# The decay matrices of a DeltaNet head in a lane of their own, with two pairs of tiles, and two tiles for the normed q

## The chip, the core and the metric

The kernel runs on one core of a Trainium2 chip. The metric is the device time of the core in microseconds (us); less is better. The engines named here are TensorE (PE; its weight loads are PEld), VectorE (DVE), ScalarE (ACT), GpSimd (POOL) and SyncE (SP), whose queue issues the DMAs.

## The reference, cut to what matters

Two transformer blocks on 512 tokens of width 1024, all in float32. Only the first block matters here. It runs grouped attention of 8 heads and, beside it, a bidirectional gated DeltaNet of 8 heads of 128, in chunks. Of one DeltaNet head and one direction (forward, and backward on the flipped sequence), with g the running sum of the log decays in a chunk:

```
decay  = exp(where(tril, g[:, None] - g[None, :], -inf))
L      = tril((k_beta @ k.T) * decay, -1)
T      = inverse of (I + L)                      # unit lower triangular
u, w   = T @ v_beta, T @ (k_beta * exp(g))
a      = (q @ k.T) * decay
# then over the chunks, one after the other
v_new  = u - w @ state
o      = (q * exp(g)) @ state + a @ v_new
state  = state * exp(g_last) + (k * exp(g_last - g)).T @ v_new
```

q and k are l2-normed, after a short convolution over the tokens and a silu.

## The kernel before

All operands are feature-major tiles of 128 x 512 (one "tile" below: 128 partitions, 512 columns, float32). A plain product of weights and activations is a `gemm` of 8 blocks; a block is three matmuls of 128x512 (step `mul`), high and low halves of both sides. 16 blocks, that is 48 `mul`, use one pair of weight tiles; the next pair is split on ACT and DVE meanwhile, and the load of the pair after that (1 MB) goes out on SP once that is done.

The function `arrange` writes one order of steps for all engines. It keeps a clock per engine from a table of costs and a list of lanes (Python generators). Between two `mul` it lets each lane whose time has come add its next step; if a product can't go on, lanes are forced. Every engine then runs its steps strictly in that order, with semaphores between the engines. So a step that is planned early on PE and whose operand is late holds all matmuls behind it.

The head loop of block 1 goes over `hd` = 0 to 7. Each turn has the products of k, the attention q, the DeltaNet q, the attention gate, v and two gates of the head before; its lanes are `att` (attention), `conv` and `con2` (convolution, silu and norm of k, q and v), `prep`, `scan` and `out`. The steps that matter, by name:

- `cv_r` i, `cv_n` i: PE sums the squares of a convolved tile (q for i = hd, k for i = 8 + hd), ACT makes the reciprocal root in two instructions, and DVE writes the normed tile (L2423): k into a tile kept by the head, q into the one tile `q_tile`.
- `g_ld` hd, d: SP loads the row of running sums of direction d, spread over the partitions, into `GS`. `pr_a`: ACT takes exp into `G_of[d]`. `pr_g`: DVE subtracts the column (4 instructions, L2432) into `B_of[d]`. `pr_e`: ACT takes exp of `B_of[d]`; POOL copies 4 columns (L3213), multiplies `q_tile` by `G_of[d]` into the kept tile `qe` (L3214), and masks `B_of[d]` (L3216).
- `pr_kk`: PE makes k k^T and q k^T (8 matmuls of 128x128 in the program, two records each in the trace); DVE multiplies both by the decays (2 and 8 instructions).
- `pr_b`, `lv_0`, then `lv_m` and `lv_x` for s = 1 to 4, `lv_e`, `lv_p1`, `lv_p2`, `lv_q1`, `lv_q2`: the triangular inverse by levels. `lv_m` and `lv_x` are 32 matmuls of 32x32 each (64 records). `lv_0` has POOL mask levels 0 and 1 (L3219, L3220); `lv_m` s < 4 has POOL mask level s + 1 (L3228), released by that `lv_m`. `lv_p1` and `lv_q1` read `B_of` once more. `lv_q2` is written back by DVE (L2487).
- `sc_v`, `sc_s`, `sc_r`, `sc_o`, `sc_oq`: the scan over four chunk pairs; POOL scales k for it (`sc_kd`, L3239). `on_b`: the norm behind it.

Before, one pair of tiles `B_of` and the one `q_tile` serve all heads. So `prep` of a head does all of `pr_a`, `pr_g`, `pr_e` itself, after both `cv_n` and after the head before has ended `lv_q2` (`work` is one slot), and only then `pr_kk`. The `cv_r` of the next q waits for `pr_kk` of the head before.

All matmuls stand at line 1833 and transposes at line 1836, since a helper records them.

Of the kernel before, what the change touches and what calls it, by code (L numbers as in the profile page):

```python
# [54 lines left out]
PRIORITY = {"tail": -2, "deca": -4, "silu": -3, "egat": -3, "att": -2, "conv": -1, "con2": -1, "scan": 0, "out": 1, "prep": 2, "gate": 3, "load": 4, "halv": 4,  # L55
# [179 lines left out]
def arrange(o, n_pairs):  # L235
# [310 lines left out]
    keep, work, acc, pads = Slots(2), Slots(1), Slots(2), Slots(4)  # L546
# [73 lines left out]
    def conv_lane(i, ip, t_in):  # L620
# [42 lines left out]
        if what == "q" and hd:  # L663
            o.behind(o.at["pr_kk", hd - 1])
# [14 lines left out]

    def prep_lane(hd):  # L680
# [9 lines left out]
        def add(kind, *key, cost, ring_=True, hold=False):  # L690
            st = banked(kind, *key, cost=cost, hold=hold) if ring_ else o.add(kind, *key, cost=cost)
            st.hd, st.keep, st.k_old, st.w_old = hd, ikeep, k_old, w_old
            return st

        for d in range(2):
            while ("g_ld", hd, d) not in o.at:
                yield
            o.behind(o.at["g_ld", hd, d])
            yield "DV"
            add("pr_a", hd, d, cost=[("AC", AC_B)], ring_=False)  # L700
            yield "DV"
            add("pr_g", hd, d, cost=[("DV", 4 * DV_S)], ring_=False)
            if hd < 7:
                t = o.now
                o.add("g_ld", hd + 1, d, cost=[("DMA", 4.0)])
                o.now = t
            yield
            add("pr_e", hd, d, cost=[("AC", AC_B), ("PO", PO_B), ("PO", PO_B)], ring_=False)
            yield "PE"
# [39 lines left out]
        work.give(0, st)  # L749

# [758 lines left out]
def build(nc, wstream, wba, consts, vecs, cossin, pos, xT, pT, outT):  # L1509
# [6 lines left out]
    with ctx:  # L1516
# [18 lines left out]
        NA = 41  # L1535
# [134 lines left out]
        B01 = A(18, 2).rearrange("p d (c n) -> p d c n", c=4)  # L1670
# [158 lines left out]
        def tensor(pe):  # L1829
# [9 lines left out]
            for q in steps:  # L1839
# [145 lines left out]
                elif kind == "pr_kk":  # L1985
                    hd = q.hd
                    w.wait_ge(sem("cv_n"), max(at["cv_n", hd].n, at["cv_n", 8 + hd].n))
                    kt_, qt_ = g4(keep_of[q.keep]["k"]), g4(q_tile)
# [28 lines left out]
                elif kind == "lv_p1":  # L2017
# [29 lines left out]
                elif kind == "lv_q1":  # L2047
# [6 lines left out]
                    for c in range(4):  # L2054
                        for d in range(2):
                            sr, ds = halves64(d)
                            i = mm(bb[ds, c, :], g4(B_of[d])[sr, c, ds], TA[sr, c, :], True, True)
# [34 lines left out]
                elif kind == "sc_oq":  # L2092
# [3 lines left out]
                    w.wait_ge(sem("pr_qe"), at["pr_e", hd, 1].n)  # L2096
# [169 lines left out]
        def vector(dve):  # L2266
# [14 lines left out]
            for q in steps:  # L2281
# [128 lines left out]
                elif kind == "cv_n":  # L2410
                    hd = q.hd
                    w.wait_ge(sem("cv_rs"), q.n)
                    if q.what == "q":
                        dst, scale = q_tile, 128.0 ** -0.5
                        if hd:
                            w.wait_ge(sem("pr_qe"), at["pr_e", hd - 1, 1].n)
                            full(at["pr_kk", hd - 1].u2)
# [7 lines left out]
                elif kind == "pr_g":  # L2425
# [5 lines left out]
                    for c in range(4):  # L2431
                        i = ts(g4(B_of[d])[:, c, :], g4(GS[:, d, :])[:, c, :], g3(gcol)[:, c, col:col + 1], 0.0,  # L2432
                               ALU.subtract, ALU.min)
                    i.then_inc(sem("pr_d"), 1)
                elif kind == "pr_kk":
# [5 lines left out]
                    for d in range(2):  # L2441
                        i = tt(K[f"AT{d}"], psum[q.u2.b][:, :], B_of[d], ALU.mult)
                    i.then_inc(drained[q.u2.b], 1)
                    empty(q.u2)
                    for d in range(2):
                        for c in range(4):
                            b_, col = g4(B_of[d])[:, c, :], d * 8 + hd
# [53 lines left out]
                elif kind == "sc_s":  # L2501
# [4 lines left out]
                    else:  # L2506
                        w.wait_ge(sem("pr_qe"), at["pr_e", hd, 1].n)
# [270 lines left out]
        def scalar(act):  # L2778
# [57 lines left out]
            for q in steps:  # L2836
# [123 lines left out]
                elif kind == "pr_a":  # L2960
                    hd, d = q.key
                    w.wait_ge(sem(f"g_ld{d}"), 16 * (hd + 1))
                    if hd:
                        w.wait_ge(sem("pr_qe"), at["pr_e", hd - 1, d].n)
                    f(G_of[d], GS[:, d, :], ACT.Exp).then_inc(sem("pr_eg"), 1)
                elif kind == "pr_e":
                    hd, d = q.key
                    w.wait_ge(sem("pr_d"), at["pr_g", hd, d].n)
                    f(B_of[d], B_of[d], ACT.Exp).then_inc(sem("pr_ed"), 1)
                elif kind == "pr_b":  # L2970
                    empty(q.u)
                    for r in Q32:
                        i = copy(dc32(hB)[r], B01[r, :, :, r])
# [219 lines left out]
        def gpsimd(po):  # L3193
# [6 lines left out]
            for q in steps:  # L3200
# [5 lines left out]
                elif kind == "pr_e":  # L3206
                    hd, d = q.key
                    LG, K, e0, D = G_of[d], keep_of[q.keep], (d * 8 + hd) * 4, B_of[d]
                    w.wait_ge(sem("pr_eg"), at["pr_g", hd, d].n)
# [3 lines left out]
                    po.tensor_copy(eglast[:, e0:e0 + 4], g4(LG)[:, :, 127 if d == 0 else 0])  # L3213
                    tt(K[f"qe{d}"], q_tile, LG, ALU.mult).then_inc(sem("pr_qe"), 1)  # L3214
                    w.wait_ge(sem("pr_ed"), q.n)
                    tt(g4(D), g4(D), bc4(C["tri_u" if d == 0 else "tri_l"]), ALU.mult).then_inc(sem("pr_ld"), 1)  # L3216
# [209 lines left out]
```

## Time and profile before

| | us |
|---|---|
| median of 3 runs | 2171.0 (2169.86 to 2171.64) |
| the profiled execution | 2173.59 |
| its span, first to last instruction | 2171.8 |
| PE busy | 2123.1 (98%) |
| DVE, ACT, POOL busy | 1251.4, 1038.6, 225.2 |
| head loop of block 1 | 41.5 to 696.5 of the span |

The page's shares are means over stages. Ends of matmuls are modelled, so what PE loses is read from its idle time, from its waits, and from the start of one instruction to the start of the next. "issue" as a releaser means that the profile shows nothing for which the engine waited. The granted clock of TensorE has two levels, 2.4 GHz (1.00) and 1.2 GHz (0.50).

### The profile page before, as it was taken

To read this page: it belongs to the slowest core of one execution; us is meant where nothing else is said; L and a number is where in the kernel's file an instruction comes from. 1 tells how busy PE (TensorE), PEld (TensorE's weight loads), DVE (VectorE), ACT (ScalarE), POOL (GpSimd) and SP (SyncE) were. 2 spreads that over 40 slices of the span, in tenths; PEclk is the share of its full clock that TensorE was granted. 3 is DMA by queue.
4 is the path that set the end of the run, shared out by engine and by line. 5 is a ranking of instruction groups with operands and counts; after the bars stand their busy time and mean duration, and the time that the engine had idled before them with its cause. 6 is when DMAs were issued, how large, how long until landed. Compare 5 with 4: busy or idle time off the path is not lost.

```text
span 2171.8 us, 35977 instructions
## 1 busy us (share of the span) xinstructions
PE 2123.1 (98%) x15046; PEld 1687.2 (78%) x15046; DVE 1251.4 (58%) x2246; ACT 1038.6 (48%) x2012; POOL 225.2 (10%) x240
## 2 busy tenths in 40 slices
PE   8999999999999999999999999999999999999999
PEld 6777676777787887877777888888777777888887
DVE  6667667666654456655556543444577766443442
ACT  6656565566655235656665332233455554322331
POOL 1112222321120000200001000000110101000000
PEclk9999999999999999999999999999999999999999
DMA  4221221221223432121111323222212112222222
GB/s 179 101 79 64 69 76 50 80 78 51 79 69 129 148 136 97 59 78 48 50 59 63 105 96 110 80 97 100 96 64 64 64 60 97 97 97 97 97 97 78
DMA packets 36227, 186.76 MB, mean 86 GB/s; under 512 B 4560, under 2 KB 4944, under 8 KB 16992
## 3 DMA queue, kind: packets, MB, share of 16 engines
q1 hardware_dynamic: 36064, 184.45, 24.7%
q8 instruction: 119, 1.95, 0.4%
q14 instruction: 44, 0.36, 0.1%
HBM read 172.86 MB, written 7.90 MB: 83 GB/s over the span
## 4 chain that ended last, share of the span: by engine, by line
PE 89%; DVE 6%; ACT 3%; issue 2%; DMA 0%; SPq 0%; POOL 0%; DVEq 0%; ACTq 0%
PE ps L1833 87%; PE ps L1836 1%; ACT arena L2781 1%; DVE spl L2287 1%; ACT spl L2784 1%; ACT hh L2781 0%; DVE x L2646 0%; DMA raw<-wstream 0%; DVE x L2404 0%; DVE arena L2589 0%; DVE x L2575 0%; DVE arena L2487 0%; DVE arena L2571 0%; DVE arena L2306 0%; DVE hl L2597 0%
## 5 line engine op out<-in xcount | busy, mean ns | idle before, releaser
L1833 PE MATMUL ps<-hh,spl 128*128 128x512 f32 (+1 forms) x3152 | 1025.2, 399 | 6.4 <-DVE hl L2579 2.1
L1833 PEld LDWEIGHTS ps<-hh,spl 128*128 128x128 f32 x3152 | 584.8, 189 | 141.2 <-issue 20.5
L1833 PE MATMUL ps<-hl,spl 128*128 128x512 f32 (+1 forms) x1568 | 619.7, 395 | 0.0
L2287 DVE TENSOR_TENSOR spl<-raw,spl 128x512 fp32r<-128x512 f32 x596 | 423.9, 735 | 157.5 <-ACT spl L2784 156.6
L1833 PE MATMUL ps<-arena_r,spl 128*128 128x512 f32 x1968 | 468.4, 392 | 10.5 <-DVE arena_r L2299 8.7
L1833 PEld LDWEIGHTS ps<-arena_r,spl 128*128 128x128 f32 x1968 | 371.7, 189 | 90.3 <-issue 10.8
L2784 ACT ACTIVATE spl<-raw 128x512 fp32r<-128x512 f32 x596 | 345.4, 620 | 142.7 <-PE ps L1833 137.5
L1833 PEld LDWEIGHTS ps<-hl,spl 128*128 128x128 f32 x1568 | 295.7, 189 | 62.9 <-issue 8.4
L1833 PE MATMUL ps<-arena 32*32 32x32 f32 (+6 forms) x5664 | 218.2, 224 | 16.4 <-issue 10.1
L2781 ACT ACTIVATE arena<-arena 128x512 f32<-128x512 f32 (+3 forms) x220 | 142.5, 649 | 189.2 <-DVE arena L2651 140.8
L1833 PEld LDWEIGHTS ps<-arena 32*32 32x32 f32 (+4 forms) x5664 | 126.1, 116 | 97.8 <-issue 79.9
L2784 ACT ACTIVATE arena_r<-arena 128x512 fp32r<-128x512 f32 x64 | 40.3, 632 | 196.0 <-DVE arena L2658 191.7
L2646 DVE TENSOR_TENSOR x<-x,ps 128x512 f32<-128x512 f32 x64 | 43.8, 685 | 133.8 <-PE ps L1833 133.8
L2781 ACT ACTIVATE arena<-ps 128x256 f32<-128x256 f32 (+5 forms) x116 | 69.0, 599 | 96.1 <-PE ps L1833 94.6
L2781 ACT ACTIVATE arena<-ps,small 128x512 f32<-128x512 f32 (+3 forms) x126 | 70.9, 566 | 77.0 <-DVE small L2747 42.8
L3250 POOL TENSOR_TENSOR arena<-arena 128x512 f32<-128x512 f32 x29 | 38.7, 1334 | 614.7 <-ACT arena L2781 614.7
L1833 PE MATMUL ps<-spl,hh 128*128 128x256 f32 x512 | 97.8, 290 | 0.7 <-ACT arena L2781 0.7
L2655 DVE TENSOR_TENSOR arena<-ps,arena 128x512 f32<-128x512 f32 x44 | 30.4, 692 | 104.3 <-PE ps L1833 104.3
L1833 PEld LDWEIGHTS ps<-spl,hh 128*128 128x128 f32 x512 | 80.1, 190 | 10.5 <-issue 8.0
L2651 DVE TENSOR_TENSOR arena<-ps,arena 128x512 f32<-128x512 f32 x44 | 30.4, 692 | 77.2 <-PE ps L1833 74.7
L1833 PE MATMUL ps<-spl,hl 128*128 128x256 f32 x256 | 72.2, 282 | 0.0
L2784 ACT ACTIVATE arena<-ps 128x256 f32<-128x256 f32 (+2 forms) x88 | 39.5, 449 | 66.4 <-PE ps L1833 51.4
(257 smaller groups left out, 2123.8 us busy)
## 6 DMA issues: line engine op xcount, KB each, us to landing
raw<-wstream SPq DMA_DIRECT2D x148, 1024.0 KB, 4.9
arena<-spill SPq DMA_DIRECT2D x17, 256.0 KB, 5.4
GS<-g_rows SPq DMA_DIRECT2D x16, 256.0 KB, 3.3
spill<-x SPq DMA_DIRECT2D x14, 256.0 KB, 2.0
arena<-arena SPq DMA_DIRECT2D x18, 128.0 KB, 2.2
x<-xT SPq DMA_DIRECT2D x4, 512.0 KB, 6.4
spill<-arena SPq DMA_DIRECT2D x8, 256.0 KB, 2.0
x<-xT SPq DMA_DIRECT2D x1, 2048.0 KB, 8.4
```

What stands on the lines that cost most here:

```text
L1833: return pe.matmul(out, lhsT, rhs, start=start, stop=stop, skip_group_check=True)
L1836: return pe.transpose(out, in_, C["ident"])
L2287: tt(spl[:, p % 2, 1, c], raw[:, p % 2, c], spl[:, p % 2, 0, c].bitcast(F32), ALU.subtract) \
L2646: tt(X[q.m], X[q.m], psum[q.u.b][:, :], ALU.add).then_inc(drained[q.u.b], 1)
L2651: tt(f_sl[q.i], psum[q.u.b][:, :], SQ[q.name][2], ALU.mult).then_inc(drained[q.u.b], 1)
L2655: tt(p, psum[q.u.b][:, :], SQ[q.g.name][2], ALU.mult).then_inc(drained[q.u.b], 1)
L2781: return act.activation(out, in_, func, **kw)
L2784: return act.activation(out, in_, ACT.Copy)
L3250: tt(acc, acc, tmp[q.i], ALU.add).then_inc(sem("sq_pool"), 1)
```

## The change

`pr_a`, `pr_g` and `pr_e` leave `prep` and form a lane `rows` of their own, with the priority of `prep`. It takes one of two pairs of decay tiles (`decs`), and waits for `g_ld` of its head and for the q product of the head before (`pr_q`), which reads `G_of`. The multiplication of q by exp(g) becomes a step of its own, `pr_q`, which `prep` adds as soon as both `cv_n` are planned; then comes `pr_kk`. A pair of decay tiles is given back at `lv_q2`. `q_tile` has two tiles, used in turn, so that `cv_r` of a q waits for the `pr_kk` of two heads before. Three tiles are added to the arena. No operation is added or removed.

```diff
-    keep, work, acc, pads = Slots(2), Slots(1), Slots(2), Slots(4)
+    keep, work, acc, pads, decs = Slots(2), Slots(1), Slots(2), Slots(4), Slots(2)
...
-        while what == "q" and hd and ("pr_kk", hd - 1) not in o.at:
+        while what == "q" and hd > 1 and ("pr_kk", hd - 2) not in o.at:
             yield
...
+    def rows_lane(hd):
+
+        while not decs.ready():
+            yield
+        decays[hd], old = decs.take()
+        o.behind(old)
+        for d in range(2):
+            while ("g_ld", hd, d) not in o.at or (hd and ("pr_q", hd - 1, d) not in o.at):
+                yield
+            o.behind(o.at["g_ld", hd, d], o.at["pr_q", hd - 1, d] if hd else None)
+            yield "DV"
+            o.add("pr_a", hd, d, cost=[("AC", AC_B)])
+            yield "DV"
+            o.add("pr_g", hd, d, cost=[("DV", 4 * DV_S)]).ib = decays[hd]
+            if hd < 7:
+                t = o.now
+                o.add("g_ld", hd + 1, d, cost=[("DMA", 4.0)])
+                o.now = t
+            yield
+            o.add("pr_e", hd, d, cost=[("AC", AC_B), ("PO", PO_B)]).ib = decays[hd]
...
         for d in range(2):
-            while ("g_ld", hd, d) not in o.at:
+            while ("pr_e", hd, d) not in o.at:
                 yield
...
-            add("pr_e", hd, d, cost=[("AC", AC_B), ("PO", PO_B), ("PO", PO_B)], ring_=False)
-            yield "PE"
+            t = o.now
+            o.behind(o.at["pr_a", hd, d])
+            add("pr_q", hd, d, cost=[("PO", PO_B)], ring_=False)
+            o.now = t
+        yield "PE"
+        o.behind(o.at["pr_e", hd, 1])
...
         work.give(0, st)
+        decs.give(decays[hd], st)
...
-        NA = 41
+        NA = 44
...
-        B_of, G_of, TM = [A(18), A(19)], [A(20), on_t[:, 1, :]], A(21)
+        B_of, G_of, TM = [[A(18), A(19)], [A(41), A(42)]], [A(20), on_t[:, 1, :]], A(21)
...
-        hC, q_tile, acc_of, dz_of = (hC0, hC1), A(25), [A(38), X[1]], [A(26), A(40)]
+        hC, q_tile, acc_of, dz_of = (hC0, hC1), [A(25), A(43)], [A(38), X[1]], [A(26), A(40)]
```

The lines of the changed file stand a little lower (1833 becomes 1852, 1836 becomes 1855). Three places show how the order moves.

On PE, `pr_kk` of head 0 (128x128 x8) before the change; its `cv_r` (pad,cst) stands 67 rows further up, 82 `mul` earlier:

```order
L1833 MATMUL ps<-hl,spl 128x512
L1833 MATMUL ps<-hh,spl 128x512 x2
L1833 MATMUL ps<-hl,spl 128x512
L1833 MATMUL ps<-hh,spl 128x512 x2
L1833 MATMUL ps<-arena 128x128 x8
L1833 MATMUL ps<-hl,spl 128x512
L1833 MATMUL ps<-hh,spl 128x512 x2
```

And after it, from that `cv_r` (pad,cst) to `pr_kk`:

```order
L1852 MATMUL ps<-pad,cst 128x512
L1852 MATMUL ps<-hh,spl 128x512
L1852 MATMUL ps<-hl,spl 128x512
L1852 MATMUL ps<-hh,spl 128x512 x2
L1852 MATMUL ps<-hl,spl 128x512
L1852 MATMUL ps<-hh,spl 128x512 x2
L1852 MATMUL ps<-hl,spl 128x512
L1852 MATMUL ps<-hh,spl 128x512 x2
L1852 MATMUL ps<-arena 128x128 x8
L1852 MATMUL ps<-arena,cst 128x512
```

`pr_kk` now stands 10 `mul` behind its `cv_r`. Over the heads the distance was 82, 70, 64, 31, 39, 40, 68, 58 `mul` and is 10, 6, 7, 10, 16, 8, 10, 15.

On PE, the first level steps of head 3 (32x32 x32 is one `lv_m` or `lv_x`), before:

```order
L1833 MATMUL ps<-arena 32x32 x32
L1833 MATMUL ps<-hl,spl 128x512
L1833 MATMUL ps<-hh,spl 128x512 x2
L1833 MATMUL ps<-hl,spl 128x512
L1833 MATMUL ps<-arena 32x32 x32
L1833 MATMUL ps<-hh,spl 128x512 x2
L1833 MATMUL ps<-hl,spl 128x512
L1833 MATMUL ps<-hh,spl 128x512 x2
L1833 MATMUL ps<-hl,spl 128x512
L1833 MATMUL ps<-arena 32x32 x32
```

And after:

```order
L1852 MATMUL ps<-x,arena 128x128 x4
L1855 MATMUL ps<-cst,x 128x128 x4
L1852 MATMUL ps<-arena 32x32 x32
L1852 MATMUL ps<-hh,spl 128x512
L1852 MATMUL ps<-hl,spl 128x512
L1852 MATMUL ps<-x,arena 128x128 x4
L1852 MATMUL ps<-arena 32x32 x32
L1852 MATMUL ps<-hh,spl 128x512
L1852 MATMUL ps<-on_t,cst 128x512
L1852 MATMUL ps<-arena 32x32 x32
```

Three of them now stand with one and two `mul` between, where there were 4 and 6, with attention steps (x,arena) and `on_b` of head 2 (on_t,cst) among them.

On POOL, head 0's copies, q products (L3214) and decay masks (L3216), then the level masks (L3219, L3220, L3228), before:

```order
L3205 TENSOR_TENSOR arena<-arena 128x512
L3213 COPY small<-arena 128x4
L3214 TENSOR_TENSOR arena<-arena 128x512
L3216 TENSOR_TENSOR arena<-arena,cst 128x512
L3205 TENSOR_TENSOR arena<-arena 128x512
L3213 COPY small<-on_t 128x4
L3214 TENSOR_TENSOR arena<-arena,on_t 128x512
L3216 TENSOR_TENSOR arena<-arena,cst 128x512
L3219 TENSOR_TENSOR arena<-arena,cst 128x256
L3220 TENSOR_TENSOR arena<-arena,cst 128x256
L3228 TENSOR_TENSOR arena<-arena,cst 128x256 x3
```

And after, from head 1's q products (now L3238), with the decay masks of head 2 (now L3229 and L3231):

```order
L3238 TENSOR_TENSOR arena<-arena 128x512
L3238 TENSOR_TENSOR arena<-arena,on_t 128x512
L3241 TENSOR_TENSOR arena<-arena,cst 128x256
L3242 TENSOR_TENSOR arena<-arena,cst 128x256
L3250 TENSOR_TENSOR arena<-arena,cst 128x256
L3229 COPY small<-arena 128x4
L3231 TENSOR_TENSOR arena<-arena,cst 128x512
L3250 TENSOR_TENSOR arena<-arena,cst 128x256
L3224 TENSOR_TENSOR arena<-arena 128x512
L3250 TENSOR_TENSOR arena<-arena,cst 128x256
L3229 COPY small<-on_t 128x4
L3231 TENSOR_TENSOR arena<-arena,cst 128x512
```

The decay masks of the next head now stand between the level masks of this one (now L3241, L3242, L3250); of the 24 masks at L3250, 6 have such a decay mask straight ahead of them or since the mask before.

## Rows read from the trace of the kernel before

**Rows 1.** The page: busy times, and the chain of waits by engine.
```profile
PE 2123.1 (98%) x15046; PEld 1687.2 (78%) x15046; DVE 1251.4 (58%) x2246; ACT 1038.6 (48%) x2012; POOL 225.2 (10%) x240
...
PE 89%; DVE 6%; ACT 3%; issue 2%; DMA 0%; SPq 0%; POOL 0%; DVEq 0%; ACTq 0%
```
**Rows 2.** Windows: block 1's head loop, then what follows; busy time of each engine.
```profile
core 0: us, PE busy (x) PEld busy (x) DVE busy (x) ACT busy (x) POOL busy (x), PEclk, DMA share, GB/s
41.50:696.50 655.00, 632.04 (x7806) 487.70 (x7805) 426.01 (x870) 396.31 (x799) 134.25 (x145) 0.99 0.22 75
696.50:800.00 103.50, 103.50 (x459) 85.69 (x458) 53.35 (x82) 33.79 (x61) 1.30 (x1) 1.00 0.45 158
```
**Rows 3.** Waits of PE in the head loop: releaser, us in total, times, longest.
```profile
PE ps L1833 <- issue: 10.1, 12, 2.7
PE ps L1833 <- DVE arena L2487: 4.6, 7, 1.2
PE ps L1833 <- DVE rv L2497: 2.2, 2, 1.7
PE ps L1833 <- DVE arena L2344: 1.4, 2, 0.8
PE ps L1833 <- ACT arena L2781: 1.1, 2, 0.7
...
PE ps L1836 <- DVE arena L2423: 0.4, 1, 0.4
```
**Rows 4.** Timeline of PE at the longest stall: start, duration, instruction, idle before.
```profile
216.40 0.74 PE L1833 MATMUL ps<-arena 32*32 32x32 f32 x64 [0.50 <-issue]
...
218.56 0.40 PE L1833 MATMUL ps<-hh,spl 128*128 128x512 f32 x1
218.89 0.70 PE L1833 MATMUL ps<-arena 32*32 32x32 f32 x59
219.82 0.25 PE L1833 MATMUL ps<-arena 32*32 32x32 f32 x5 [0.23 <-issue]
...
223.42 0.62 PE L1833 MATMUL ps<-arena 32*32 32x32 f32 x48
226.71 0.43 PE L1833 MATMUL ps<-arena 32*32 32x32 f32 x16 [2.67 <-issue]
...
228.53 0.63 PE L1833 MATMUL ps<-hl,spl 128*128 128x512 f32 x1
```
**Rows 5.** The page, DMA queues: the queue that brings instructions.
```profile
q8 instruction: 119, 1.95, 0.4%
```
**Rows 6.** Timeline of the DMA issues on SP beside that stall.
```profile
219.19 0.33 SPq L1750 DMA_DIRECT2D raw<-wstream  x1
219.57 0.44 SPq L1771 DMA_DIRECT2D spill<-x  x1
```
**Rows 7.** Windows around that stall; the column behind POOL's is the granted clock.
```profile
218.00:224.00 6.00, 5.77 (x191) 4.04 (x190) 4.08 (x7) 2.62 (x6) 2.18 (x4) 1.00 0.60 186
224.00:227.00 3.00, 0.33 (x20) 0.28 (x15) 0.00 (x0) 0.00 (x0) 0.34 (x1) 0.76 0.19 70
225.00:232.00 7.00, 5.29 (x89) 3.93 (x89) 2.10 (x4) 1.50 (x3) 0.00 (x0) 0.54 0.01 2
```
**Rows 8.** Timeline, heads 0 and 1: cv_r on PE, and cv_n on DVE.
```profile
93.64 1.03 PE L1833 MATMUL ps<-pad,cst 128*128 128x512 f32 x2
...
96.09 0.69 DVE L2423 SCALAR_TENSOR_TENSOR arena<-x,pad 128x512 f32<-128x512 f32 x1 [0.82 <-ACT pad L2781]
...
174.11 1.02 PE L1833 MATMUL ps<-pad,cst 128*128 128x512 f32 x2
...
177.99 0.68 DVE L2423 SCALAR_TENSOR_TENSOR arena<-x,pad 128x512 f32<-128x512 f32 x1
```
**Rows 9.** Groups of POOL by line in the head loop: count, busy time, mean ns.
```profile
L3228 POOL TENSOR_TENSOR arena<-arena,cst 128x256 f32<-128x256 f32 x24 | 23.8, 997 | 35.6 <-PE ps L1833 27.4 <-DVE arena L2456 8.2
L3216 POOL TENSOR_TENSOR arena<-arena,cst 128x512 f32<-128x512 f32 x16 | 22.0, 1377 | 38.3 <-ACT arena L2781 38.3
...
L3214 POOL TENSOR_TENSOR arena<-arena,on_t 128x512 f32<-128x512 f32 x8 | 10.3, 1293 | 0.0
...
L3213 POOL COPY small<-on_t 128x4 f32<-128x4 f32 x8 | 1.9, 234 | 31.6 <-ACT on_t L2781 31.6
```
**Rows 10.** Timeline of POOL: the level masks of head 1.
```profile
216.37 2.24 POOL L3228 TENSOR_TENSOR arena<-arena,cst 128x256 f32<-128x256 f32 x2 [1.02 <-DVE arena L2456]
222.44 0.74 POOL L3228 TENSOR_TENSOR arena<-arena,cst 128x256 f32<-128x256 f32 x1 [3.82 <-PE ps L1833]
```
**Rows 11.** The view of DMAs, head loop: loads of weights: count, KB each, us to landing.
```profile
raw<-wstream SPq DMA_DIRECT2D x33, 1024.0 KB, 5.0
```

More of the change, by code:

```diff
@@ L54 @@
 MARGIN_1 = 0.0
-PRIORITY = {"tail": -2, "deca": -4, "silu": -3, "egat": -3, "att": -2, "conv": -1, "con2": -1, "scan": 0, "out": 1, "prep": 2, "gate": 3, "load": 4, "halv": 4,
+PRIORITY = {"tail": -2, "deca": -4, "silu": -3, "egat": -3, "att": -2, "conv": -1, "con2": -1, "scan": 0, "out": 1, "prep": 2, "rows": 2, "gate": 3, "load": 4, "halv": 4,
             "rope": 5}
@@ L662, in conv_lane @@
             yield "PE"
-        if what == "q" and hd:
-            o.behind(o.at["pr_kk", hd - 1])
+        if what == "q" and hd > 1:
+            o.behind(o.at["pr_kk", hd - 2])
         st = banked("cv_r", i, cost=[("PE", PE_B), ("AC", AC_B), ("AC", AC_B)])
@@ L678, in conv_lane @@
             st.keep = kept[hd]
+    decays = {}
+    def rows_lane(hd):
[17 more added lines that the diff above has]
+            o.add("pr_e", hd, d, cost=[("AC", AC_B), ("PO", PO_B)]).ib = decays[hd]
     def prep_lane(hd):
@@ L691, in add @@
             st = banked(kind, *key, cost=cost, hold=hold) if ring_ else o.add(kind, *key, cost=cost)
-            st.hd, st.keep, st.k_old, st.w_old = hd, ikeep, k_old, w_old
+            st.hd, st.keep, st.k_old, st.w_old, st.ib = hd, ikeep, k_old, w_old, decays[hd]
             return st
         for d in range(2):
-            while ("g_ld", hd, d) not in o.at:
+            while ("pr_e", hd, d) not in o.at:
                 yield
[L698 to L707, printed above, removed]
-            add("pr_e", hd, d, cost=[("AC", AC_B), ("PO", PO_B), ("PO", PO_B)], ring_=False)
-            yield "PE"
+            t = o.now
[4 more added lines that the diff above has]
+        o.behind(o.at["pr_e", hd, 1])
         while not ring.ready(2):
@@ L827, in arrange @@
         o.spawn("att", att_lane(hd))
+        o.spawn("rows", rows_lane(hd))
         o.spawn("prep", prep_lane(hd))
@@ L1669, in build @@
         X01 = [A(9 * i + 3, 2).rearrange("p d (c n) -> p d c n", c=4) for i in range(2)]
-        B01 = A(18, 2).rearrange("p d (c n) -> p d c n", c=4)
+        B01 = [A(i, 2).rearrange("p d (c n) -> p d c n", c=4) for i in (18, 41)]
         def two(u, n):
@@ L2095, in tensor @@
                         w.wait_ge(drained[q.ou.b], q.ou.n - 1)
-                    w.wait_ge(sem("pr_qe"), at["pr_e", hd, 1].n)
+                    w.wait_ge(sem("pr_qe"), at["pr_q", hd, 1].n)
                     for d in range(2):
@@ L2413, in vector @@
                     if q.what == "q":
[L2414 to L2417, printed above, removed]
+                        dst, scale = q_tile[hd % 2], 128.0 ** -0.5
+                        if hd > 1:
+                            w.wait_ge(sem("pr_qe"), at["pr_q", hd - 2, 1].n)
+                            full(at["pr_kk", hd - 2].u2)
                     else:
@@ L2506, in vector @@
                     else:
-                        w.wait_ge(sem("pr_qe"), at["pr_e", hd, 1].n)
+                        w.wait_ge(sem("pr_ld"), at["pr_e", hd, 1].n)
                         for d in range(2):
@@ L2963, in scalar @@
                     if hd:
-                        w.wait_ge(sem("pr_qe"), at["pr_e", hd - 1, d].n)
+                        w.wait_ge(sem("pr_qe"), at["pr_q", hd - 1, d].n)
                     f(G_of[d], GS[:, d, :], ACT.Exp).then_inc(sem("pr_eg"), 1)
@@ L2968, in scalar @@
                     w.wait_ge(sem("pr_d"), at["pr_g", hd, d].n)
-                    f(B_of[d], B_of[d], ACT.Exp).then_inc(sem("pr_ed"), 1)
+                    f(B_of[q.ib][d], B_of[q.ib][d], ACT.Exp).then_inc(sem("pr_ed"), 1)
                 elif kind == "pr_b":
@@ L2972, in scalar @@
                     for r in Q32:
-                        i = copy(dc32(hB)[r], B01[r, :, :, r])
+                        i = copy(dc32(hB)[r], B01[q.ib][r, :, :, r])
                     i.then_inc(sem("pr_b"), 1)
@@ L3207, in gpsimd @@
                     hd, d = q.key
-                    LG, K, e0, D = G_of[d], keep_of[q.keep], (d * 8 + hd) * 4, B_of[d]
-                    w.wait_ge(sem("pr_eg"), at["pr_g", hd, d].n)
+                    e0, D = (d * 8 + hd) * 4, B_of[q.ib][d]
+                    w.wait_ge(sem("pr_eg"), at["pr_a", hd, d].n)
+                    po.tensor_copy(eglast[:, e0:e0 + 4], g4(G_of[d])[:, :, 127 if d == 0 else 0])
+                    w.wait_ge(sem("pr_ed"), q.n)
+                    tt(g4(D), g4(D), bc4(C["tri_u" if d == 0 else "tri_l"]), ALU.mult).then_inc(sem("pr_ld"), 1)
+                elif kind == "pr_q":
+                    hd, d = q.key
+                    w.wait_ge(sem("pr_eg"), at["pr_a", hd, d].n)
                     if q.k_old:
```

17 lines of the change are left out of this document (7 added, 10 removed).

## The prediction, made before the changed kernel had run

> **What bounds the kernel now.** I read the page first. PE is busy 98% of the span and makes 89% of the chain of waits, and POOL, which the change moves most, is busy 10% [rows 1]. So the change can give only what PE idles in block 1's head loop, and what PE's clock loses there. The windows bound that: from 41.5 to 696.5 us PE is busy 632.0 of 655.0 us, so 23.0 us are idle; behind the loop, from 696.5 to 800, it idles not at all, though the last head's chain still runs there [rows 2]. An earlier end of that chain is worth nothing.
>
> The waits of PE split the 23.0 us [rows 3]. (a) 4.6 us, 7 times, for DVE's write-back of `lv_q2` (L2487): `sc_v` stands one `mul` behind `lv_q2`. (b) 10.1 us, 12 times, "issue". Three of the twelve, 2.3 us, stand ahead of the first `lv_m` of heads 1, 4 and 6 (the 0.50 us at 216.40 is one, [rows 4]): PE was early for `lv_0`. The other nine, 7.8 us, stand inside a level step, where nothing is to be waited for: 59 records of 32x32, a gap of 0.23, then 5; or 48, a gap of 2.67, then 16 [rows 4]. (c) The rest, 8.3 us, is scattered over other releasers, none over 2.2 us in total.
>
> The nine gaps are waits for instructions. The instruction queue brought 1.95 MB in 119 packets [rows 5], 16.4 KB each; the program has 30,499 PE instructions (two to each of the 15046 matmul records [rows 1], and 407 others), which is 256 to a packet and 64 bytes each. Counting along the built order, every one of the nine gaps stands 193 or 194 instructions beyond a multiple of 256: where a new packet begins. A level step burns 128 instructions in 0.7 us [rows 4], a `mul` two in 103.5/459 = 0.23 us [rows 2]. The packet needed at 219.82 came 3.4 us after the one before was begun at 216.40; the next came 6.9 us after 219.82, since a 1 MB load and a spill went out at 219.19 and 219.57 [rows 6] and held the DMA engines 60% busy [rows 7]. After the 2.67 us PE ran at the lower level: 0.54 granted over 225 to 232, 1.00 before [rows 7], so 0.46 x 7.0 = 3.2 us at the higher level are lost, unless other waits hid them.
>
> **The change part by part.** The sum is made against the profiled execution's span, 2171.8 us (2173.59 as timed, 2.6 above the median of 2171.0; I carry the difference over to the median).
>
> 1. PE's own work: the same 11,723 matmuls. Changes from `mul` to another step or back are 470 instead of 472 in the loop; one costs 0.33 (218.56 to 218.89 [rows 4]) less 0.23, 0.1 us. Sum -0.2; bounds -1 and +1, as which kinds meet also changes.
>
> 2. What leaves the path ahead of `pr_kk`. No row of PE's waits names POOL or the decays [rows 3]: `pr_kk` never waited for them, since the planner placed it late enough. So the order gets earlier, not the waits shorter: 0. The `lv_q2` to `sc_v` distance is one `mul` again in seven heads: 4.6 us stay. From `pr_kk` to the first `lv_m` the durations of the rows between add up to 8.4 to 11.3 us before and 8.5 to 14.5 after: the 2.3 us stay, within 1 either way.
>
> 3. The new neighbour: `pr_kk` stands 6 to 16 `mul` behind its q's `cv_r` instead of 31 to 82. From the start of `cv_r`, by the durations of what stands between, it is due after 3.6, 3.5, 4.9, 3.6, 4.5, 4.0, 3.1 and 4.3 us (mean 3.9). It needs ACT's two steps and `cv_n`. That took 96.78 - 93.64 = 3.1 us for head 0 and 178.67 - 174.11 = 4.6 for head 1, where other work was ahead on DVE [rows 8]; over the eight, 3.1 to 6.0, mean 4.2. Head by head the excess is 3.4 us in sum, the upper bound. The lower one is 0: `tr_k` stands as close behind `cv_r` of k and waited once, 0.4 us (L2423 [rows 3]), because the planner knows what is queued. Nearer is that row, the same instruction in the same role: +0.5.
>
> 4. POOL. Pool's q product and decay mask are split: 1.29 and 1.38 us, with 0.23 for the copy [rows 9]. `pr_q` now heads POOL when `lv_0` comes; its 2 x 1.29 us end well before `pr_kk` has gone through DVE. But 6 of 24 level masks get a decay mask ahead: 1.38 + 0.23 = 1.6 us and, if ACT is late with its exp, that too. The level mask takes 1.0 [rows 9] and is released by `lv_m`; from there to the next `lv_m` lie about 1.1 us of `mul`, 0.7 of `lv_x` and 1.6 of `mul`, 3.4 us. 3.4 - 1.0 - 1.6 leaves 0.8 us as cover (before, POOL idled 3.82 us ahead of such a mask [rows 10]). Bounds 0 and 6 x 1.6 = 9.6; nearer the idle POOL: +0.5.
>
> 5. SP. `g_ld` is issued earlier and waits for `pr_a` and `pr_g`; weight loads are queued behind it. A load goes out about 13 `mul` before its pair of tiles is used up by the pair before, lands in 5.0 us [rows 11] and has a further 48 `mul`, 11 us, until its products. 0; +1 at worst.
>
> 6. Instruction packets. By the same durations, stretches of 256 instructions shorter than 3.4 us are five before (2.4, 2.4, 2.8, 2.9, 3.1) and four after (2.8, 2.8, 3.1, 3.3). A weight load goes out at `mul` 30 to 44 of 48. The 2.67 us fell on a stretch of 3.9 us begun at `mul` 36. After, the 3.1 is begun at 39 (head 3, where level steps stand one and two `mul` apart), and stretches of 4.2, 4.0 and 4.4 us at 38, 34 and 32. The two of 2.8 cost 3.4 - 2.8 each, 1.2. The 3.1 costs 0.3 without a load and 6.9 - 3.1 = 3.8 with one; I take 2. The three others cost 0 to 2.7 each; I take 1.5, for the one like case cost 2.67 and a stretch of 4.2 begun at 36 in head 6 cost nothing. 1.2 + 2 + 4.5 = 7.7 against 7.8: 0, bounds 1.5 - 7.8 = -6.3 and 13.1 - 7.8 = +5.3.
>
> On this the Trainium skill says otherwise: its page "Runtime: NRT & Kernel Launch" (Instruction fetch mechanics) has instructions come in blocks of 256, and crossing a block mostly hidden. The size agrees with rows 5, the hiding does not with the gaps in rows 4. By that rule point 6 would be 0 with no spread, and the two rivals that rest on it would have hardly a chance.
>
> 7. The clock: a gap of the 2.67 kind is as likely as before, in head 3 instead of 1. 0; -3.2 without one, +3.2 with a second.
>
> Sum: -0.2 + 0.5 + 0.5 = +0.8 us: 2171.8.
>
> **The rivals.** (A) The long gap dissolves: no packet is begun in the 2 us round a load's issue with a short stretch behind it. Gain 2.7 - 0.3 and 3.2 of clock, with 0.5 of other gaps: -6.1, 2164.9. For it: it took one coincidence in eight heads. Against: four candidates now.
>
> (B) Slower: `pr_kk` waits on PE for `cv_n`, and with it all `mul` queued behind. The price is 8 x (latency - 3.9). It passes 0.2% from a mean latency of 4.5 us; at 5, as with two more DVE steps ahead, it is 8 x 1.1 = 8.8 less what the clock doesn't notice: 2179.8. For it: heads 1, 2, 4 and 7 took 4.4 to 6.0 before. Against: `tr_k`.
>
> (C) Slower by packets: one more gap of 2.7 us and its 3.2 us of clock, +5.9: 2176.9. For: the dense steps of head 3. It is A turned round.
>
> (D) That the change doesn't do what it says is excluded: the built order has the decay steps of the next head among this head's levels.
>
> **How the numbers follow.** A measurement of this kernel can tell about 0.2%, 4.3 us. The forecast (within 0.2%) gets 0.56, A 0.21, B 0.12, C 0.11. So faster 0.21, same 0.56, slower 0.23. The range takes in A and most of B: 2164 to 2180.
>
> **What the changed profile would show.** PE busy unchanged within 2 us in total. L2487 among PE's waits with some 4.6 us. A new row of PE for L2423 at `pr_kk`: under 1 us, or over 4 if B. No row naming POOL above 1 us. Gaps inside level steps: 5 to 13 us in sum, the longest in head 3; none over 1.5 us and the clock at 1.00 through the loop if A. Wrong would be an idle time in the loop under 16 or over 32 us, or a change behind it.

## The result, and the profile of the changed kernel

The changed kernel took 2178.3 us (median of 10 runs, 2171.2 to 2182.9) against 2171.5 us for the kernel before on the same chip (10 runs, 2169.9 to 2174.9): a ratio of 1.0027, 95% interval 1.0018 to 1.0036. Ratios here and below come from all fast runs of both kernels together, so they differ a little from the quotient of the medians, here 1.0031. That is slower, by a little more than the 0.2% that I called measurable. Its profiled execution took 2177.99 us with a span of 2176.2, 4.4 us more than that of before.

The page of the changed kernel, busy times and chain, to be held against [rows 1]:

```profile
PE 2123.8 (98%) x15046; PEld 1688.8 (78%) x15046; DVE 1243.6 (57%) x2246; ACT 1039.9 (48%) x2012; POOL 223.3 (10%) x240
...
PE 89%; DVE 5%; ACT 3%; issue 2%; DMA 1%; POOL 0%; SPq 0%; DVEq 0%; ACTq 0%; POOLq 0%
```

Nothing to see there: the same work, the same bound. The window of the head loop, which is now 658.9 us long from its first to its last product, where it was 655.1, and the windows behind its two longest stalls (the granted clock stands behind POOL's column, as in [rows 2] and [rows 7]):

```profile
41.50:701.00 659.50, 633.15 (x7809) 489.30 (x7807) 423.78 (x877) 402.19 (x807) 133.28 (x145) 0.99 0.23 78
701.00:800.00 99.00, 99.00 (x438) 81.98 (x437) 46.62 (x72) 27.81 (x50) 0.00 (x0) 1.00 0.40 140
...
318.00:322.00 4.00, 4.00 (x70) 2.64 (x71) 1.25 (x2) 2.60 (x5) 0.73 (x1) 0.59 0.01 4
...
556.00:563.00 7.00, 5.27 (x121) 3.79 (x121) 2.39 (x8) 1.42 (x3) 0.93 (x2) 0.76 0.01 3
```

PE idles 659.5 - 633.2 = 26.3 us in the loop, 3.3 more than the 23.0 of [rows 2], and behind it not at all, as before. What it waits for in that window, beside [rows 3] (releaser, us in total, times, longest):

```profile
PE ps L1852 <- issue: 11.1, 11, 2.5
PE ps L1852 <- DVE arena L2506: 5.0, 7, 1.2
PE ps L1852 <- DVE rv L2516: 3.2, 2, 1.9
PE ps L1852 <- ACT pad L2803: 2.0, 2, 1.3
PE ps L1852 <- POOL kdt L3261: 1.6, 1, 1.6
...
PE ps L1855 <- DVE arena L2442: 0.4, 1, 0.4
```

Counted apart, record by record along the built order as for the prediction: gaps at a packet boundary (instruction 193 or 194 beyond a multiple of 256) were 7.8 us in 9 places and are 10.1 us in 9 places. All other gaps in the loop were 15.1 us and are 16.2. The two long packet gaps now stand in heads 3 and 6 (timeline of PE: start, duration, instruction, idle before):

```profile
315.23 0.50 PE L1852 MATMUL ps<-hh,spl 128*128 128x512 f32 x1
317.93 1.37 PE L1852 MATMUL ps<-on_t,cst 128*128 128x512 f32 x2 [2.20 <-issue]
...
554.85 0.38 PE L1852 MATMUL ps<-arena 32*32 32x32 f32 x21
557.73 0.85 PE L1852 MATMUL ps<-arena 32*32 32x32 f32 x43 [2.50 <-issue]
```

and the timeline of SP has a 1 MB load 4.6 and 5.3 us ahead of the start of either gap:

```profile
311.17 0.33 SPq L1769 DMA_DIRECT2D raw<-wstream  x1
...
549.92 0.33 SPq L1769 DMA_DIRECT2D raw<-wstream  x1
```

The trace also has the transfers of the instruction queue (q8 on the page, 119 packets of 16 KB), and they bear the counting out. PE entered the packet before the gap of head 3 at 312.41. From then to 315.7 no instruction packet was moved, but 0.95 MB of other data; the packet came as soon as that had ended (the view of DMAs, 312.4 to 315.7, then 315.7 to 316.8: queue, packets, MB, share of 16 engines):

```profile
q1 hardware_dynamic: 131, 0.95, 73.3%
...
q8 instruction: 1, 0.02, 5.4%
```

Its transfer took 0.95 us, to 316.70, and PE went on at 317.93, 1.23 us later. In all 92 packet gaps over 0.2 us that the table below counts, over its fourteen traces, PE went on 1.20 to 1.60 us after the end of such a transfer.

So the 3.8 us of the loop are 2.3 of packet gaps, 1.1 of other waits and 0.4 of PE's own time. The median rose by 6.8 us, the profiled execution by 4.4, and the ten runs show how: at a mean granted clock of 1.000 the changed kernel took 2171.2 us, at 0.998 2174.7 to 2176.7, at 0.997 2178.0 and 2178.7, at 0.995 2180.7 and 2181.9, at 0.993 2182.7 and 2182.9.

### The profile page after: what moved, and what is told of

Read it like the earlier page. It is cut to its first block, busy times and chain, and to the rows that moved or that the text cites. A ratio compares the mean times of both kernels' runs of the same rounds, so it can differ in the third digit from the quotient of the medians.

```text
span 2176.2 us, 35967 instructions
## 1 busy us (share of the span) xinstructions
PE 2123.8 (98%) x15046; PEld 1688.8 (78%) x15046; DVE 1243.6 (57%) x2246; ACT 1039.9 (48%) x2012; POOL 223.3 (10%) x240
## 4 chain that ended last, share of the span: by engine, by line
PE 89%; DVE 5%; ACT 3%; issue 2%; DMA 1%; POOL 0%; SPq 0%; DVEq 0%; ACTq 0%; POOLq 0%
PE ps L1852 88%; PE ps L1855 1%; ACT arena L2800 1%; DVE spl L2306 1%; ACT spl L2803 1%; ACT hh L2800 0%; DVE x L2665 0%; DMA raw<-wstream 0%; DVE arena L2608 0%; DVE x L2594 0%; DVE arena L2590 0%; DMA arena<-spill 0%; DVE arena L2325 0%; DVE hl L2616 0%; DVE arena L2506 0%
## 5 line engine op out<-in xcount | busy, mean ns | idle before, releaser
L1852 PE MATMUL ps<-arena 32*32 32x32 f32 (+6 forms) x5664 | 219.0, 225 | 14.7 <-issue 8.9
```

The source lines that it names most:

```text
L1852: return pe.matmul(out, lhsT, rhs, start=start, stop=stop, skip_group_check=True)
```

## The experiments

Two theories. **P**: the time went into later instruction packets, long ones while a 1 MB load is in flight, and into half-clock stretches behind long gaps. **W**: it went into the new waits between engines. Every kernel from a0 on was timed in five rounds beside the kernel before. The table reads one profiled execution of each; "packet gaps" is their sum in us, with their number and the longest in brackets; "half clock" is the time in the loop in which the clock records show the lower level.

| kernel | ratio, 95% interval | packet gaps | other gaps | half clock | loop |
|---|---|---|---|---|---|
| before | 1 | 7.8 (9; 2.7) | 15.1 | 6.8 | 655.1 |
| changed | 1.0027 [1.0018, 1.0036] | 10.1 (9; 2.5) | 16.2 | 6.8 | 658.9 |
| a0 changed, again | 1.0036 [1.0024, 1.0048] | 10.2 (10; 2.3) | 16.3 | 10.2 | 660.8 |
| a1 changed +168 | 0.9995 [0.9986, 1.0004] | 5.3 (8; 1.5) | 15.8 | 6.8 | 653.8 |
| a2 changed +48 | 1.0054 [1.0040, 1.0068] | 12.8 (8; 3.4) | 15.8 | 23.9 | 668.0 |
| c3 changed +256 | 1.0054 [1.0042, 1.0066] | 10.2 (9; 2.3) | 15.9 | 20.5 | 664.7 |
| a3 before +120 | 0.9976 [0.9966, 0.9986] | 4.3 (7; 1.2) | 16.2 | 0 | 649.9 |
| c1 changed, light loads | 0.9957 [0.9945, 0.9969] | 0.6 (2; 0.5) | 14.5 | 3.4 | 645.0 |
| c2 before, light loads | 0.9981 [0.9973, 0.9990] | 5.7 (10; 1.3) | 14.7 | 0 | 649.5 |
| d1 changed, quarter loads | 0.9961 [0.9950, 0.9973] | 2.6 (6; 1.3) | 14.6 | 3.4 | 647.8 |
| d2 before, quarter loads | 0.9978 [0.9969, 0.9988] | 5.7 (8; 1.5) | 13.0 | 3.4 | 649.5 |
| d4 changed, one q tile | 1.0026 [1.0017, 1.0035] | 10.9 (8; 2.2) | 15.7 | 10.2 | 660.5 |
| c4 before, scan yields, +208 | 0.9985 [0.9975, 0.9995] | 5.5 (6; 2.3) | 12.9 | 17.1 | 653.2 |
| d3 changed, scan yields, quarter | 0.9965 [0.9952, 0.9977] | 4.9 (5; 1.3) | 12.3 | 0 | 644.6 |

Take from each loop its two kinds of gaps and half of its time at half clock: 626 to 629 us are left in all of them. So these three things make the difference between the kernels, but for at most 3 us.

### Moving the packet boundaries

The instructions are untouched, but a few tiny matmuls stand at the start of PE's program, four PE instructions each. Here there are 42 of them, 168 instructions; 12 make 48, 30 make 120 and 64 make 256:

```diff
             w.wait_ge(sem("ld_vec"), 32)
+            for _ in range(42):
+                mm(psum[7][0:32, 0:32], C["ident"][0:32, 0:32], C["ident"][0:32, 0:32], True, True)
```

The changed kernel as it is:

> The changed kernel again, beside the kernel before on the same chip, as the base of the next three. Theory P (instruction packets): PE's idle time in the head loop rose by 3.5 us, of which the gaps at the start of an instruction packet make 2.3 (7.8 before, 10.1 after, the 2.2 us ahead of on_b of head 2 among them); the rest of the 5.8 us is TensorE's clock, which falls to 1.2 GHz behind long gaps. It expects 2175 to 2181 us, ratio 1.002 to 1.004, and runs with a lower granted clock to be the longer ones. Theory W (waits between engines): the new waits for POOL, DVE and ACT (1.6, 1.9, 1.3 us) make it; it expects the same time here.

> The changed kernel with 42 small matmuls (168 PE instructions with their weight loads) at the start of the program, where PE waits for its first operands; nothing else differs, but each packet of 256 instructions now begins 168 instructions earlier in the work. From the starts of PE's instructions in the trace of the changed kernel, no stretch of 256 in the loop is then both short and begun at a weight load. Theory P: packet gaps in the loop fall from 10.1 to about 3 us, none over 1 us, the clock stays at 1.00 in the loop: 2166 to 2172 us, faster than the changed kernel by 6 to 12. Theory W: the waits between engines are the same, 2175 to 2181 us.

> The changed kernel with 12 small matmuls (48 PE instructions) at the start. Theory P: by the same count the packet gaps in the loop come to about 14 us, in several gaps over 2 us: 2181 to 2190 us, slower than the changed kernel by 3 to 10. Theory W: 2175 to 2181 us, no difference.

> The kernel before with 30 small matmuls (120 PE instructions) at the start. Theory P: packet gaps in the head loop fall from 7.8 to about 2 to 4 us and the 2.7 us gap with its stretch at 1.2 GHz goes: 2160 to 2167 us, ratio 0.995 to 0.998 to the kernel before. Theory W: 2171 us, as before.

Medians were 2179.47, 2172.35, 2185.62 and 2168.66 us, against 2173.34 for the kernel before. The same instructions in the same order differ by 13 us with the place at which packets begin. Packet gaps and half-clock time differ with it, the other gaps don't (15.8 to 16.3). Theory W has nothing for this. Theory P had the order of the four right and +48 in its numbers, but was too hopeful for the two others: +168 kept 5.3 us of packet gaps, the longest 1.5, and 6.8 us at half clock, where I expected about 3, none over 1 and a full clock, and its time is 0.4 us above the range; +120 kept 4.3 us where I expected 2 to 4, and is 1.7 us above its range. For +48 the longest gap, in head 6, is no longer inside a level step but between products (timeline of PE):

```profile
558.40 0.39 PE L1852 MATMUL ps<-hl,spl 128*128 128x512 f32 x1
562.22 0.74 PE L1852 MATMUL ps<-hh,spl 128*128 128x512 f32 x2 [3.43 <-issue]
```

One could still say that any displacement, or a later start of the loop, is what helps. A shift by one whole packet answers that:

> The changed kernel with 256 more PE instructions (64 tiny matmuls) at its start: one whole packet. Theory P: the boundaries fall on the same instructions as without them, so the same gaps: 10 us at packet boundaries in 9 places, the long ones in heads 3 and 6, 2178 to 2182 us. Rival S (any displacement or the later start of the loop was what helped with 168): 2172 to 2175 us.

It took 2183.17 us (before: 2171.87). The gap in head 6 is back at the very instruction, 21 of 64 records into the level step (timeline of PE):

```profile
561.12 0.38 PE L1852 MATMUL ps<-arena 32*32 32x32 f32 x21
563.80 0.85 PE L1852 MATMUL ps<-arena 32*32 32x32 f32 x43 [2.30 <-issue]
```

The time is 1 us above the bound of what P expected: the 64 extra matmuls start the loop 3.4 us later (at 45.26 instead of the 41.86 us of a0), which I had not put into the numbers. +168 starts it 1.6 us later (43.46), so it gains more than its ratio shows.

### Taking the loads out of the packets' way

Here PE's instructions and packet boundaries are untouched. First the 33 weight loads of the head loop are made small. These two kernels leave most of the weights out and compute wrong results; only their times are used:

```diff
-                    sp.dma_start(raw[:, p % 2, :], wstream[p]).then_inc(sem(f"ld_w{p % 2}"), 16)
+                    if 5 <= p < 38:
+                        sp.dma_start(raw[:, p % 2, 0:64], wstream[p][:, 0:64]).then_inc(sem(f"ld_w{p % 2}"), 16)
+                    else:
+                        sp.dma_start(raw[:, p % 2, :], wstream[p]).then_inc(sem(f"ld_w{p % 2}"), 16)
```

> The changed kernel with its instructions untouched; only the 33 weight loads of block 1's head loop carry 64 of their 2048 columns each (32 KB instead of 1 MB), so that the products of those pairs are made with stale weights. Theory P (gaps are waits for packets of 256 PE instructions, long ones where a 1 MB load is in flight, and half-clock stretches follow them): gaps at packet boundaries fall from 10.2 us to under 3, none over 1.3, and the half-clock stretches behind them go; about 7 us less of gaps and 3 to 5 of clock: 2166 to 2171 us, ratio 0.997 to 0.999 to the kernel before. Theory W (the time went into new waits between engines): the gaps of engine waits stay at 16 us under either theory, and by W the time stays at 2176 to 2180.

> The kernel before with the same 33 light loads (stale weights). Theory P: packet gaps from 7.8 us to under 3, none long, no half-clock stretch behind one: 2162 to 2168 us. The distance to the changed kernel with light loads is then what the change costs without the packets: by P 0 to 2 us (1.1 us of engine waits, and what a half-clock stretch behind one of them costs), by W still 5 to 7 us.

Medians: 2162.90 us for the changed kernel, 2167.45 for the kernel before with light loads, 2171.87 for the kernel before. PE's waits in the loop of the changed kernel with light loads (its lines are 3 lower):

```profile
PE ps L1855 <- DVE arena L2509: 5.0, 7, 1.2
PE ps L1855 <- ACT pad L2806: 2.0, 2, 1.3
PE ps L1855 <- DVE rv L2519: 1.9, 1, 1.9
PE ps L1855 <- POOL kdt L3264: 1.6, 1, 1.6
PE ps L1855 <- issue: 1.4, 3, 0.7
```

"issue" fell from 11.1 to 1.4 us, the releasers that are engines kept their numbers, but for one wait for `rv` of 1.3 us. At the place in head 3, PE's timeline runs through:

```profile
311.99 0.50 PE L1855 MATMUL ps<-hh,spl 128*128 128x512 f32 x1
312.33 1.02 PE L1855 MATMUL ps<-on_t,cst 128*128 128x512 f32 x2
```

W is refuted as the main cause. But P missed too, in two numbers. The changed kernel gained more than expected (3 us below the range), and the kernel before kept 5.7 us of packet gaps where I expected under 3. So the loads cost 7.8 - 5.7 = 2.1 us of gaps before and 10.2 - 0.6 = 9.6 after: the gaps of the changed kernel are nearly all collisions with a load. Without the loads the sign turns: the changed kernel is then 4.5 us faster, not slower.

That sign holds for this one position of the packets. Where a stretch of 256 instructions is too short for its packet and no load is in front, PE goes on 3.1 us at the soonest after it began the stretch (3.05 us from 566.95 to 570.00 in the changed kernel, 3.42 from 216.40 to 219.82 in [rows 4]). If I lay the boundaries at each of the 256 possible positions in turn, by the instruction starts of c2 and c1, and sum what the stretches lack of the prediction's 3.4 us, I get 2.3 us for the kernel before and 2.4 for the changed one in the mean, from 0.2 to 4.9 and from 0.2 to 5.8, and 2.8 and 1.6 at the position of these runs. That is an estimate, no run, and a rough one: a stretch of 2.8 us at 256.77 in the changed kernel cost nothing. By it the lane has no advantage in short stretches; at this position it happens to have one. Neither kernel with light loads was run at another position.

The transfers also show that "short stretch" is not the whole of the 5.7 us. Five of the gaps of c2, 3.2 us in sum (1.05, 0.78, 0.39, 0.49 and 0.51), stand on stretches of 3.9 to 4.6 us, gap left out. All five come at the boundary right behind another gap, and their packets began to move only 2.4 us after PE had crossed into the packet before. In the kernel c1 this took 0.7 us in head 3 and 1.1 in head 6. So one late packet often has another behind it. Why is open; behind two other gaps of c2 it took 1.2 and 1.3 us.

That suggested a remedy that computes everything. Each quarter of a weight tile is free as soon as it is split, so the load can go out in four parts, 6 `mul` apart:

```diff
                 if q.kind == "load":
                     p = q.key[0]
+                    if 5 <= p < 38:
+                        continue
...
+                elif q.kind == "w_lo" and 5 <= q.key[0] + 2 < 38:
+                    p, a = q.key[0] + 2, q.key[1]
+                    sp.wait_ge(sem("w_lo"), q.n)
+                    sp.dma_start(raw[:, p % 2, 512 * a:512 * a + 512], wstream[p][:, 512 * a:512 * a + 512]) \
+                        .then_inc(sem(f"ld_w{p % 2}"), 16)
```

ACT waits for 64 instead of 16 increments of such a pair; that line is left out here.

> The changed kernel, complete, PE's order untouched: each of the 33 weight loads of the head loop goes out as four of 256 KB, each as soon as its quarter of the tile is split (6 mul apart), not as one of 1 MB behind the fourth. If packets are late because a whole 1 MB load is ahead of them, a quarter ahead costs them a quarter: packet gaps fall from 10.2 us to 1 to 4, none over 1.5, engine waits stay at 15 to 16 us, 2164 to 2170 us, ratio 0.996 to 0.999. If it is the bytes in flight as such, wherever they lie, the gaps stay at 8 to 11 us and the time at 2176 to 2180.

> The kernel before with the same 33 loads in four parts. It has 5.7 us of packet gaps even with light loads and 7.8 with whole ones, so 5.5 to 7.5 us of them stay, and 2167 to 2171 us. With d1 it shows the sign of the change once the loads are out of the packets' way: by the light loads the changed kernel should come out 0 to 5 us faster, where it is 6 slower with whole loads.

Medians: 2163.89 and 2167.79 us, against 2172.56 for the kernel before. The gap in head 6 of the changed kernel is at the same instruction and half as long, that in head 3 went from 2.20 to 0.50 us (timeline of PE):

```profile
312.23 0.50 PE L1859 MATMUL ps<-hh,spl 128*128 128x512 f32 x1
313.24 1.13 PE L1859 MATMUL ps<-on_t,cst 128*128 128x512 f32 x2 [0.50 <-issue]
...
548.54 0.38 PE L1859 MATMUL ps<-arena 32*32 32x32 f32 x21
550.16 0.57 PE L1859 MATMUL ps<-arena 32*32 32x32 f32 x43 [1.25 <-issue]
```

Both times are as expected but for 0.1 us of d1, which is that much below its range. The same bytes in spaced parts give most of what leaving them out gave, so it isn't the traffic as such, it is one whole load in front of a packet. The transfers say the same. From PE's crossing into the packet before to the start of the transfer it took, with whole, quarter and light loads, 3.3, 1.4 and 0.7 us at the gap in head 3, and 4.4, 3.2 and 1.1 us at the one in head 6. The changed kernel with quarter loads is the fastest complete version of the study by its median, 0.39% faster than the kernel before (interval 0.27 to 0.50), and 3.9 us faster than the kernel before with the same loads. Here too the second comparison was made at one position of the packets only.

### The parts of the change, and the wait behind `lv_q2`

The lane alone, with one q tile:

> The lane of decays alone: as changed, but one q tile, cv_r of a q behind pr_kk of the head before again. The planner then writes the very same order of steps (pr_kk of a head is planned before the next q is convolved), so nothing should move: packet gaps 10 us, engine waits 16 us, 2178 to 2181 us. If the second tile is worth something, DVE's cv_n would wait here for POOL's q product and PE's tr or pr_kk for it: 1 us or more in new rows, 2181 to 2186.

2178.79 us, the order of PE's instructions is that of the changed kernel, and so are the waits. The second q tile does nothing, good or bad: the planner never had to wait for it. All of the change's effect comes from the lane.

The one large wait that both kernels share, `sc_v` one `mul` behind `lv_q2`, has its cause in the planner: the scan lane adds its first step without asking whether its time has come. I gave it that question:

```diff
         o.behind(o.at["lv_q2", hd], o.at["tr_v", hd], o.at["tr_k", hd])
+        yield "PE"
```

> The kernel before with one more wait for the planner's clock ahead of the scan's first step, so that sc_v stands 2 to 8 mul behind lv_q2 instead of 1 (4.6 us of PE's waits lay there), and with 208 more PE instructions at the start, a phase in which the rows of the kernel before give few short packets. Theory P with the wait term as in the prediction: the row of waits at lv_q2's write-back falls under 0.5 us, packet gaps 3 to 6 us, 2162 to 2168 us, ratio 0.995 to 0.998. Rival: the waits turn up at other steps, other gaps stay at 15 to 16 us: 2168 to 2172.

> d1 with one more wait for the planner's clock ahead of the scan's first step: sc_v stands 3 to 6 mul behind lv_q2 instead of 1, in another order of PE's steps. A version meant to beat both: 5.0 us of waits at lv_q2 go, 1 to 3 come elsewhere (as in the run of the kernel before with it), packet gaps 1 to 5 us: 2160 to 2167 us. If new waits eat it, 2167 to 2172.

2169.55 us (before: 2171.87; single runs from 2162.5 to 2174.9), 1.6 us above what P expected, and 2164.48 us (before: 2172.56), in its range. The packet gaps of c4 were as expected, 5.5 us; its time is the rival's, though the other gaps did not stay at 15 to 16. The profiled execution was the slowest of twelve, with 17.1 us at half clock, so its row in the table is not typical. In both the row of `lv_q2`'s write-back is gone, and the order that results has others. PE's waits in the loop of d3:

```profile
PE ps L1860 <- issue: 6.9, 9, 1.3
PE ps L1860 <- DVE arena L2420: 2.8, 2, 2.1
PE ps L1860 <- ACT pad L2811: 2.1, 2, 1.4
PE ps L1860 <- ACT x L2808: 2.1, 3, 0.7
```

Other gaps fell by 2.3 us to 12 or 13, half of what the removed row held. In d3 the packet gaps took the 2.3 back (4.9 instead of d1's 2.6), so it is no faster than d1. It was meant to beat d1 and did not.

## The prediction, point by point

The time lay in the range (2178.3 in 2164 to 2180), but the likeliest case, within 0.2%, was not what came: it was slower by 0.27%. What came is nearest to rival C, slower by packets with their clock, 2176.9, which had a chance of 0.11; but C had one more gap of 2.7 us with a half-clock stretch, and the profiled execution has 2.3 us more in several gaps and as much time at half clock as before. That the range held is partly luck: its upper end was set by rival B, which did not happen. Nothing of the explanation of the kernel before had to be taken back: PE idle in the loop was the right place, and behind the loop nothing changed.

1. **PE's own work.** Forecast -0.2, bounds 1 either way; busy in the loop rose by 1.1 us in a window with three records more. Right within its bounds.
2. **Waits before `lv_m` and `sc_v`.** The row of L2487, now L2506, is 5.0 instead of 4.6 us, as forecast. The early `lv_m` did not stay at 2.3 us but fell to 0.9, 0.4 more than I had allowed.
3. **`pr_kk` close behind `cv_r`.** It now stands 3.2 to 5.1 us behind it, and no wait of `pr_kk` for `cv_n` is among PE's waits; the one row of L2442 is that of `tr_k`, as before. 0 instead of +0.5, and rival B is refuted. The nearest row had been the right guide.
4. **POOL.** Level masks are not waited for by PE. But I had looked at level masks alone, and the decay mask stands ahead of a third kind of POOL's work: the k scaled for the scan. The timeline of POOL in the changed kernel,

```profile
426.40 1.28 POOL L3231 TENSOR_TENSOR arena<-arena,cst 128x512 f32<-128x512 f32 x1 [5.56 <-ACT arena L2800]
427.67 1.18 POOL L3261 TENSOR_SCALAR kdt<-arena,small 128x128 f32<-128x128 f32 x2
```

and that of PE beside it:

```profile
426.99 0.40 PE L1852 MATMUL ps<-hl,spl 128*128 128x512 f32 x1
428.99 0.68 PE L1852 MATMUL ps<-rv,kdt 128*128 128x128 f32 x4 [1.61 <-POOL kdt L3261]
```

POOL began the mask of head 5 at 426.40, 1.27 us before it could turn to head 4's `kdt`, and `sc_s` waited 1.61. It happened once in eight heads. My "no row naming POOL above 1 us" was wrong by this row.

Points 2 to 4 together were to bring +1.0 us of waits between engines, and the other gaps rose by 1.1. That the sum was right is luck, for its members were not: `kdt` +1.6, `rv` +1.0 and waits for ACT against gains at `lv_m` and elsewhere. In a0, where the order is the same, each such wait has the same length within 0.1 us; these are properties of the order.

5. **SP and weight loads.** As forecast, no wait of PE for them.
6. **Instruction packets.** This is the step that failed: 7.7 us forecast, 10.1 measured. The mechanism was right and the list of places was not. The stretches that I had priced cost less than I gave them: the two of 2.8 us 0.2 instead of 1.2; head 3, where I had put the long gap, 2.20 us for my 2; the three others, begun at `mul` 38, 34 and 32, 0.96, 1.44 and 0 instead of 4.5. Together that is 4.8 us for my 7.7. The other 5.3 us came at five boundaries for which I had nothing: 2.50 (head 6) and 1.30, both begun at `mul` 44, 0.42 at 42, 0.64 at 45 and 0.47 at 3. The first three were begun 1.2 to 2.0 us after a load was issued, which is within the "2 us round a load's issue" that rival A names; why they were not among the candidates I can't say. By the light loads 9.6 us of 10.2 are due to loads, where I had 1.7 + 4.5 = 6.2. Short stretches by themselves, for which I had 1.5 us, cost 0.6 after but 5.7 before, and of the latter 3.2 is a late packet behind a late packet, which the working did not have at all. So against before, loads take 7.5 us more and the rest gives 5 back, both by where packets happen to begin.
7. **The clock.** In the profiled execution equal, 6.8 us at half clock in either, now as two stretches of 3.4. In the median it was not: the 2.4 us by which the median rose more than the profiled execution go with the clock, as the ten runs show. That more long gaps give it more occasions fits this, but was not tried. The half-clock time of a0 (10.2) and c3 (20.5), with nearly the same gaps, says how widely this varies; my bounds of 3.2 were those of one stretch.

Of the signs that I had named, PE busy (0.7 us more), L2487, the idle time (26.3 us) and the sum of packet gaps came as said. The longest gap was in head 6, not 3, and the one in head 3 stands between a product and `on_b`, not inside a level step.

On the Trainium skill's rule (page "Runtime: NRT & Kernel Launch", Instruction fetch mechanics) that crossing a block is mostly hidden: the loop has 2 x 7806 / 256 = 61 crossings, of which nine show a gap in either kernel, so by number the rule holds. By price it does not in this kernel: it would have had no difference between a1 and a2, and 13 us were measured.

## What to carry to other kernels

When two versions of a kernel differ by less than half a per cent and an engine runs thousands of small instructions, time each with its instructions displaced by two or three parts of a packet before a cause is looked for in the edit: here one and the same order gave 0.9995, 1.0036 and 1.0054 of the kernel before. A large load that is issued beside such a dense stretch should go out in spaced parts; here that cost a few lines and gave more (0.9961) than the new placement of steps in c4 (0.9985). And where a step moves to another engine's queue, go through every kind of work in that queue that someone waits for, not only the kind it was moved away from.

## What the runs showed of the hardware

- How late a packet of 256 PE instructions comes depends on what is ahead of it. Its transfer of 16 KB took 0.96 us in the median once begun, and PE went on 1.20 to 1.60 us after its end (92 gaps). At one and the same boundary in head 6 PE stood still for 2.0 to 2.5 us with a 1 MB load ahead, for 1.25 us with 256 KB parts, and not at all with light loads; in head 3 for 2.2, 0.5 and 0 us. The longest gap of all was 3.4 us (+48).
- Half-clock stretches come in lengths of 3.4 us or twice that, 17 of them in the loops of a0, a2, c3 and d4 together. They follow gaps of 1.4 us and more, whatever the cause, or several shorter ones close together (0.5, 0.7 and 0.6 us from 146 to 150 in a0), but not each time. The wait of 1.89 us for `rv` in head 3 is the same in the changed kernel and in d1. Behind it the clock stayed in the first, at 350.75 (windows of the changed kernel),

```profile
344.00:351.00 7.00, 4.59 (x28) 3.56 (x28) 5.50 (x9) 4.12 (x9) 4.34 (x4) 1.00 0.12 40
351.00:358.00 7.00, 7.00 (x41) 5.20 (x41) 4.74 (x12) 3.90 (x9) 2.52 (x3) 1.00 0.00 0
```

and fell in the second, from 344.8 (windows of d1):

```profile
341.00:345.00 4.00, 2.11 (x15) 1.55 (x13) 3.96 (x6) 2.46 (x5) 4.00 (x4) 1.00 0.00 0
344.00:348.00 4.00, 3.06 (x12) 2.87 (x13) 2.83 (x6) 1.25 (x3) 1.95 (x2) 0.63 0.20 66
```

What decides between the two was not tried and stays open. The spread between runs of one kernel goes with it (a0: 2178.6 to 2184.1 us at 0.996 and 0.994). Open too is why a packet behind a late packet is sometimes late itself.
